# Two layers of a hybrid language model on one core: the head of the program regrouped, gates and squares scaled before the down projections, their sums added on VectorE, the last norm applied through row sums

## The reference

```python
def rmsnorm(x, g):
    xf = x.astype(jnp.float32)
    var = jnp.mean(xf * xf, axis=-1, keepdims=True)
    return (xf * lax.rsqrt(var + EPS) * g.astype(jnp.float32)).astype(x.dtype)
# first block, layer l
xn = rmsnorm(h, norm_mix_g[l])
u = jnp.einsum('bsd,de->bse', xn, w_in[l])
q, k, v, xr, gr, ga, gb = jnp.split(u, splits, axis=-1)
...
hn = rmsnorm(h, norm_ffn_g[l])
g, up = jnp.split(hn @ w_ffn_in[l], 2, axis=-1)
h = h + (jax.nn.silu(g) * up) @ w_ffn_out[l]
# second block, after each mixer, with a rmsnorm of its own:
#   h = h + relu(hn @ w_up) ** 2 @ w_down, and at the end rmsnorm(h, final_norm_g)
```

## Time and profile before

| | |
|---|---|
| time, median of 3 runs (lowest to highest) | 1148.96 us (1147.88 to 1152.42) |
| the profiled execution: its own time, its span | 1151.9 us, 1150.2 us |
| mean granted TensorE clock | 0.996 |
| busy: PE, DVE, ACT, POOL | 1121.5, 757.2, 573.3, 228.5 us |
| moved by DMA | 187.32 MB, mean 163 GB/s |

### The profile page before, as it was taken

How to read it: one execution, slowest core, us unless ns; L and a number is a source line. 1 busy time by engine, 2 the same in 40 slices (tenths; PEclk the granted TensorE clock), 3 DMA queues, 4 the chain that set the end, 5 groups by cost and what they waited for, 6 DMA issues and landing times.

```text
span 1150.2 us, 21081 instructions
## 1 busy us (share of the span) xinstructions
PE 1121.5 (98%) x8516; PEld 1070.6 (93%) x8516; DVE 757.2 (66%) x933; ACT 573.3 (50%) x747; POOL 228.5 (20%) x227
## 2 busy tenths in 40 slices
PE   6999999999999999999999999999989999999997
PEld 6999899999888899999999988899989999889996
DVE  5747884666777743699886777753367657776333
ACT  6346556635655543565664555543345445554331
POOL 1996001402000000267844010000030002000001
PEclk9999999999999999999999999999999999999999
DMA  9574433654665555446410355555545445555531
GB/s 282 178 250 145 161 112 111 219 181 151 204 197 184 182 189 180 142 131 195 154 38 2 111 183 182 186 197 179 181 134 183 147 148 183 183 182 188 181 142 37
DMA packets 154947, 187.32 MB, mean 163 GB/s; under 512 B 6496, under 2 KB 143872, under 8 KB 154880
## 3 DMA queue, kind: packets, MB, share of 16 engines
q1 hardware_dynamic: 151312, 184.06, 49.0%
q10 hardware_dynamic: 3568, 2.31, 0.7%
HBM read 185.29 MB, written 1.07 MB: 162 GB/s over the span
## 4 chain that ended last, share of the span: by engine, by line
PE 88%; DVE 8%; ACT 1%; DMA 1%; issue 1%; SPq 0%; POOLq 0%; POOL 0%; DVEq 0%
PE PS L441 17%; PE PS L383 17%; PE PS L384 17%; PE PS L385 17%; PE PS L443 9%; DVE WL L379 2%; DVE XHL L538 1%; PE PS L1936 1%; PE PS L1949 1%; PE PS L730 1%; DMA RAW<-in_w_in 1%; DVE QKV L1532 1%; PE PS L1898 1%; PE PS L680 1%; PE PS L1824 1%
## 5 line engine op out<-in xcount | busy, mean ns | idle before, releaser
L379 DVE TENSOR_TENSOR WL<-RAW,WH 128x2048 fp32r<-128x2048 f32 x171 | 400.5, 2343 | 215.9 <-ACT WH L370 215.9
L370 ACT ACTIVATE WH<-RAW 128x2048 fp32r<-128x2048 f32 x171 | 326.6, 1911 | 225.6 <-PE PS L385 206.9
L441 PE MATMUL PS<-XHL,WH 128*128 128x512 f32 x864 | 300.9, 395 | 0.0
L383 PE MATMUL PS<-XHL,WH 128*128 128x256 f32 x832 | 242.0, 291 | 13.6 <-DVE WL L332 6.9
L443 PE MATMUL PS<-XHL,WL 128*128 128x256 f32 x864 | 239.6, 277 | 0.0
L384 PE MATMUL PS<-XHL,WH 128*128 128x256 f32 x832 | 236.8, 285 | 0.0
L385 PE MATMUL PS<-XHL,WL 128*128 128x256 f32 x832 | 236.7, 284 | 0.0
L441 PEld LDWEIGHTS PS<-XHL,WH 128*128 128x128 f32 x864 | 162.1, 188 | 37.4
L383 PE MATMUL PS<-HH,WH 128*128 (+1 forms) x688 | 194.7, 283 | 0.0
L385 PE MATMUL PS<-HH,WL 128*128 (+1 forms) x688 | 194.7, 283 | 0.0
L384 PE MATMUL PS<-HL,WH 128*128 (+1 forms) x688 | 194.7, 283 | 0.0
(11 more groups left out here) (296 smaller groups left out, 1605.5 us busy)
## 6 DMA issues: line engine op xcount, KB each, us to landing
RAW<-in_mlp_w_up SPq DMA_DIRECT2D x32, 1024.0 KB, 5.4
RAW<-in_mlp_w_down SPq DMA_DIRECT2D x32, 1024.0 KB, 5.0
RAW<-in_w_in SPq DMA_DIRECT2D x26, 1024.0 KB, 5.2
RAW<-in_w_ffn_in_pairs SPq DMA_DIRECT2D x22, 1024.0 KB, 5.1
RAW<-in_dn_w_in SPq DMA_DIRECT2D x16, 1024.0 KB, 5.7
RAW<-in_mb_w_in SPq DMA_DIRECT2D x12, 1024.0 KB, 5.2
RAW<-in_w_ffn_out SPq DMA_DIRECT2D x11, 1024.0 KB, 5.0
RAW<-in_w_attn_out SPq DMA_DIRECT2D x4, 1024.0 KB, 5.3
```

The source lines that it names most:

```text
L370: act.activation(WH[:, k], RAW[:, k], ACT.Copy).then_inc(hi_done, 1)
L379: dve.tensor_tensor(WL[:, k], RAW[:, k], WH[:, k].bitcast(F32), ALU.subtract).then_inc(lo_done, 1)
L383: pe.matmul(out, wh, xh, start=start, stop=False, skip_group_check=True)
L441: pe.matmul(out.rearrange("p (e t) -> p e t", e=2), h[:, k, part], XHL[:, :, k], start=(k == 0), stop=False, skip_group_check=True)
```

## The change

The head: `xr` 2 is fetched and split in quarters too, `xr` 3 and `qk` 0 are fetched before the bias rows and `WRI`, ten matmuls of `ONES` are issued on PE as soon as `ONES` is set, ACT takes the norm's root before it splits `xr` 3, and DVE inverts it before its own split; the rows are made after the second quarter of `xr` 2. In the attention the low part of `gr` 1 is made between shift and scale of the first pair, that of `gr` 2 after its scale, and the scans come one chunk later. The decay rows get banks 6, 7, 4, 5 and are made together ahead of `dq` 9; the key and query sums move to banks 6 and 7. In `fi` both halves, and in `u0` and `u1` the relu, are multiplied by the rows before the product or the square (ACT squares twice: rounded, and in full), `ROWS_AT` for `u0` and `u1` goes from 5 to 3, and the down projections' banks are added to `H` by DVE directly. `w1` has its last block in bank 4, so that the last pair of blocks is finished block by block; the last norm has its sums in token columns, its root on two columns, and its rows through PE.

```diff
+        WARM = 10
+            pe.wait_ge(s_.const, 1)
+            for _ in range(WARM):
+                pe.matmul(PS[:, 7, 0:P], ONES[:], ONES[:], start=True, stop=True)
             for st in (Step(seg["xr"], j, None) for j in range(4)):
-                if st.j < 2:
+                if st.j < 3:
                     multiply_pieces(pe, st)
...
+                if c == 2 and p == 1:
+                    norm_point(pe, 0, 4)
...
-            for p in range(4):
-                fetch_piece(sp, 1, p)
-            fetch(sp, Step(seg["xr"], 2, None))
+            for c in (1, 2):
+                for p in range(4):
+                    fetch_piece(sp, c, p)
+            fetch(sp, Step(seg["xr"], 3, None))
+            fetch(sp, Step(seg["qk"], 0, None))
             sp.wait_ge(s_.ext_ready, 1)
...
             for st in (Step(seg["xr"], j, None) for j in range(4)):
-                split_hi(act, st)
                 if st.j == 1:
                     norm_root(act, 0)
+                if st.j:
+                    split_hi(act, st)
...
-                split_lo(dve, st)
-                attn_scale(dve, ch, n)
+                if n:
+                    split_lo(dve, st)
+                    attn_scale(dve, ch, n)
+                else:
+                    split_lo(dve, Step(seg["v"], 3, None))
+                    attn_scale(dve, ch, n)
+                    split_lo(dve, st)
...
-                if n < 4:
-                    scan(n)
+                if 0 < n < 5:
+                    scan(n - 1)
...
-        ROWS_AT = [4, 3, 2, 5, 3, 5]
+        ROWS_AT = [4, 3, 2, 3, 3, 3]
...
+        def add_rows(dve, sg, m):
+            for b in range(4 if m != FINAL else 3):
                 if b < 3:
                     dve.wait_ge(s_.rows_done, 3 * h4_no[sg.name] - 2 + b)
                 else:
                     dve.wait_ge(mm_done, sg.first + sg.n)
-                dve.tensor_tensor(XN[:, 2 * b:2 * b + 2, :], PS[:, b, :].rearrange("p (c t) -> p c t", c=2), by_rows(2),
-                                  ALU.mult).then_inc(s_.rows_scaled, 1)
-                if b > 1 and m != FINAL:
-                    norm_low(dve, m, b - 2)
                 hb = H[:, 2 * b:2 * b + 2, :]
-                ins = pool.tensor_tensor(hb, hb, XN[:, 2 * b:2 * b + 2, :], ALU.add)
+                ins = dve.tensor_tensor(hb, hb, PS[:, b, :].rearrange("p (c t) -> p c t", c=2), ALU.add)
...
+                if b and m != FINAL:
+                    norm_low(dve, m, b - 1)
...
+            dve.wait_ge(s_.rows_done, 3 * h4_no[sg.name] + 1)
+            dve.tensor_tensor(H[:, KB - 2], H[:, KB - 2], PS[:, 3, 0:TOK], ALU.add).then_inc(s_.h4, 1)
+            dve.wait_ge(mm_done, sg.first + sg.n)
+            dve.tensor_tensor(H[:, KB - 1], H[:, KB - 1], PS[:, 4, 0:TOK], ALU.add).then_inc(s_.h4, 1)
...
+                def square_of(st):
+                    k = slot_of(st, -1)
+                    act.wait_ge(s_.sg_in, st.local(base_ - 1))
+                    act.activation(hid(HH, st, 2, 1), two(SG[:, k]), ACT.Square).then_inc(s_.hh_done, 1)
+                    act.wait_ge(s_.hl_done, st.local(base_ - 4))
+                    act.activation(HP[:, k], SG[:, k], ACT.Square).then_inc(s_.hp_done, 1)
...
             def decay_rows(g):
-                if g >= 2:
-                    pe.wait_ge(s_.b_read, g - 1)
                 pe.wait_ge(s_.gc_done, 1)
-                rows_of(GC, 4 * g, 6 + g % 2).then_inc(s_.b_done, 1)
+                rows_of(GC, 4 * g, GB[g]).then_inc(s_.b_done, 1)
...
+        def final_pieces(act):
+            for p in range(3):
+                norm_high(act, FINAL, p)
+                if p < 2:
+                    final_scaled(act, p)
+            for j in (KB - 2, KB - 1):
+                act.wait_ge(s_.h4, h4_no["w1"] + j - (KB - 2))
+                act.activation(XN[:, j], H[:, j], ACT.Square).then_inc(s_.sq_done, 1)
+            final_scaled(act, 2)
+        def final_scaled(act, p):
+            for j in (2 * p, 2 * p + 1):
+                ins = act.activation(OUTG[:, j], H[:, j], ACT.Copy, scale=weight(FINAL, j))
+            ins.then_inc(s_.outg, 1)
...
-            ch(dve.reciprocal(RSTD[:], RH[:]))
-            ch.wait(dve)
+            dve.reciprocal(RC[:, 0:2], SDC[:, 0:2]).then_inc(s_.rc_ready, 1)
+            dve.wait_ge(s_.rows_ready, FINAL + 1)
             for p in range(4):
...
+                blk = slice(2 * p, 2 * p + 2)
+                dve.wait_ge(s_.outg, p + 1)
+                dve.tensor_tensor(XN[:, blk], OUTG[:, blk], PS[:, 5, None, 0:TOK].to_broadcast([P, 2, TOK]),
+                                  ALU.mult).then_inc(s_.xout, 1)
```

More of the change, by code:

```diff
@@ L252, in build @@
         x_in = [sem(f"x_in{p}") for p in range(4)]
-        piece_in = [sem(f"piece_in{p}") for p in range(6)]
+        piece_in = [sem(f"piece_in{p}") for p in range(9)]
         hi_done = sem("hi_done")
@@ L465, in multiply_rows @@
                 xl = HL[:, bass.ds(st.rel * KROWS + k, 1), :].rearrange("p k t -> p (k t)")
-                mm = product(pe, PS[:, b // 2, (b % 2) * TOK:(b % 2 + 1) * TOK],
+                if st.seg.name == "w1" and b == KB - 1:
+                    if first and k == 0:
+                        c = seg["u1"].first + seg["u1"].n - 1
+                        pe.wait_ge(freed[c % SLOTS], c // SLOTS + 1)
+                    out, opens = PS[:, 4, 0:TOK], first and k == 0
+                else:
+                    out, opens = PS[:, b // 2, (b % 2) * TOK:(b % 2 + 1) * TOK], first and k == 0 and b % 2 == 0
+                mm = product(pe, out,
                              h[:, k, b * P:(b + 1) * P], l[:, k, b * P:(b + 1) * P], xh, xl,
-                             first and k == 0 and b % 2 == 0, last and k == KROWS - 1)
-                if last and b % 2 and b < KB - 1 and k == KROWS - 1:
+                             opens, last and k == KROWS - 1)
+                if last and b < KB - 1 and k == KROWS - 1 and (b % 2 or st.seg.name == "w1" and b == KB - 2):
                     mm.then_inc(s_.rows_done, 1)
@@ L556, in norm_sums @@
             if m == FINAL:
[L557 to L560, removed]
+                pe.wait_ge(s_.sq_added, 6)
+                for j in (0, 1, 4, 5, 6, 7):
+                    if j >= 4:
+                        pe.wait_ge(s_.sq_done, 4 * m + max(j - 2, 3))
+                    for c in range(TT):
+                        mm = pe.matmul(PS[:, 6 + c, 0:P], XN[:, j, c * P:(c + 1) * P], ONES[:], start=(j == 0), stop=(j == 7),
+                                       skip_group_check=True)
             elif m == 2:
@@ L580, in norm_root @@
             elif m == FINAL:
-                act.activation(RH[:], PS[:, 4, 0:TOK], ACT.Sqrt, bias=EPSC[:], scale=1.0 / D).then_inc(s_.sd_done, 1)
+                act.activation(SDC[:, 0:2], PS[:, 6:8, 0], ACT.Sqrt, bias=EPSC[:], scale=1.0 / D).then_inc(s_.sd_done, 1)
             else:
@@ L819, in _ @@
                                  a[w].rearrange("(j e) d f -> e d j f", e=2)[e]).then_inc(s_.wri_in, 16)
-            fetch(sp, Step(seg["xr"], 3, None))
-            for name, n in SEGMENTS[1:]:
+            for st in (Step(seg["qk"], j, None) for j in range(1, 8)):
+                fetch(sp, st)
+            for name, n in SEGMENTS[2:]:
                 steps(sp, seg[name], lambda st: fetch(sp, st))
@@ L1015, in add_halves @@
             dve.tensor_tensor(two(SG[:, st.slot]), two(SG[:, st.slot]), wide_sides(st)[0], ALU.add).then_inc(freed[st.slot], 1)
-        def squares_ready(earlier):
-            def ready(act, st):
-                act.wait_ge(s_.hp_done, st.local(earlier - 1))
-            return ready
         @block.scalar
@@ L1040, in _ @@
             squares(act, 0, 3)
+            for p in range(4):
+                split_hi_piece(act, 2, p)
             def late_inputs():
@@ L1406, in _ @@
             for st in (Step(seg["xr"], j, None) for j in range(4)):
+                if st.j == 0:
+                    for p in range(4):
+                        split_lo_piece(dve, 2, p)
+                    continue
+                if st.j == 1:
+                    norm_inverse(dve, 0)
                 split_lo(dve, st)
-                if st.j == 0:
-                    continue
                 if st.j == 1:
@@ L1509, in up @@
                 dve.wait_ge(freed[st.slot], st.uses())
-                dve.tensor_tensor(SG[:, st.slot, 0:TOK], SG[:, st.slot, 0:TOK], RSTD[:], ALU.mult).then_inc(s_.sg_in, 1)
+                dve.tensor_tensor(two(SG[:, st.slot]), two(SG[:, st.slot]), by_rows(2), ALU.mult).then_inc(s_.sg_in, 1)
                 if st.i is not None or st.j >= 1:
@@ L2078, in _ @@
             norm_sums(pe, FINAL)
+            pe.wait_ge(s_.rc_ready, FINAL + 1)
+            for c in range(TT):
+                mm = pe.transpose(PS[:, 5, c * P:(c + 1) * P], RC[:, c:c + 1].to_broadcast([P, P]), IDENT[:])
+            mm.then_inc(s_.rows_ready, 1)
 _VECTORS = [name for name, _ in VECTORS]
```

112 lines of the change are left out of this document (55 added, 57 removed).

## The result

The changed kernel takes 1134.67 us (median of 4 runs, 1133.43 to 1135.08), against 1149.81 us for the kernel before beside it (4 runs, 1147.88 to 1152.42): a ratio of 0.9867, interval 0.9855 to 0.9879, or 15.1 us less. The forecast was 1129.5 in a range of 1125.0 to 1136.0; the sign and the range hold, the range by 1.3 us, and the size was overrated by a quarter. The profiled execution of the changed kernel has a span of 1133.4 us and an own time of 1135.08, 0.4 above its median. That of before stood some 2.1 above the median given here, so the two spans differ by 16.8 us where the medians differ by 15.1.

What follows compares the result with a forecast made beforehand. PE, busy 98% of the span, was taken as the bound. Gains of 5.4 + 3.6 + 7.2 + 1.1 + 4.2 = 21.5 us cut the span from 1150.2 to 1128.7; the median forecast was 1129.5, range 1125 to 1136.

Steps and rivals of the forecast that it cites:

- The head's wait and its low clock: Head: PE's wait for the norm's rows and the low clock after it go, gaining 5.4 us, bounds 1.5 and 6.2.
- the first pair's: First head pair: PE's 2.05 us wait and the 1.5 us low clock go, together 3.6 us, bounds 1.8 and 3.8.
- `fo`'s waits: End of `fo`: two of PE's six waits for low parts go, gaining 2.2 us of the down projections' 7.2.
- the decay rows': Decay rows: the 1.09 us wait goes but PE next waits for ACT's squares; gain 1.1 us, bounds 0.4 and 1.7.
- No wait of PE over 0.2 us between 7 and 550 us: One of the signs that would show the prediction right, for PE between 7 and 550 us.
- 1.8 us of `ROWS_AT`: Earlier `ROWS_AT`: root, half sums and inverse take some 1.8 us of DVE's 2.8; cost 0, at worst 0.5 twice.
- The step that failed: `w0`: End of `w0`: four of PE's six waits for low parts go, with a later one on `mq` 1, gaining 5.0 us.
- The tail: End of the kernel: finishing the last blocks and norm sooner gains 4.2 us, bounds 3.0 and 5.0.
- (a): Rival: a handoff behind the old wait takes its place, above all in the head; about 1136 us, chance 0.22.
- (b): Rival at the start: the ten dummy matmuls hold the clock up; 1128.7 us, chance 0.10.
- (c): Rival: PE's stalls don't add up, as DVE keeps its old times in `dq` and `dz`; 1140 us, chance 0.03.
- (d): Rival: slower, as the squares of `u0` and `u1` close a ring within a chunk; about 1210 us, chance 0.02.

Runs made afterwards that it cites:

- sums on DVE: The changed kernel with the sums of squares after `w0` (norm 4) on DVE and no longer on POOL: 1131.60 us, ratio 0.9841.
- the head alone: The kernel before with only the new order of the head, without dummies: 1146.23 us against 1149.69, ratio 0.9963.
- no dummies: The changed kernel without its ten dummy matmuls at the start: 1134.72 us, ratio 0.9866 to the kernel before.
- fewer sums: The changed kernel with DVE adding squares of blocks 1 to 0 and 5 to 4, so the last norm's sums take 16 records, not 24: 1133.90 us, 0.9856.
- the third square: The changed kernel with one more ACT square, into a tile nothing reads, in each chunk of `u0` and `u1`: 1134.55 us, ratio 0.986.
- pair alone: The kernel before with only the new order around the first head pair: 1145.86 us, ratio 0.9971.

## Why the prediction was right, and where its sum was off

**Right, by the runs.** PE was what bound the kernel, and the change paid where PE had stood still or run slowly. The head's wait and its low clock went (5.2 of 5.4 at `xr` 3), the first pair's too (3.5 of 3.6, and 3.5 when it was done alone), `fo`'s waits (2.4 of 2.2), the decay rows' (0.9 of 1.1, and 0.9 when undone). The new queue of transfers in the head cost nothing, nor did the doubled scaling in `fi` or the squares on ACT in `u0` and `u1`. "No wait of PE over 0.2 us between 7 and 550 us" failed by one wait, that of 0.3 us for a convolution, which the prediction had named among the signs of being wrong. How the gain of a place divides among the edits made there together (fetches, quarters and order in the head; blocks, columns and scaling in the tail) was not taken apart. The table load that the prediction packs into 1.8 us of `ROWS_AT` takes 1.28 us by itself in the trace; no wait came of it. And its count of the low windows, "17 and 16 matmuls start", is of those that overlap them: 15 and 14 start.

**The step that failed: `w0`, 5.0 predicted, 2.9 measured.** The prediction laid the new chain of DVE's adds and low parts against PE's quarters and found a lead of 1 us. It priced the low parts as with POOL idle, since the row adds were gone. POOL's adds of squares stayed. Before, DVE's low parts met POOL's instructions at this place and the two splits behind them did not (they start at 852.44 and take 4.48 us together). The prediction had the row in hand: low parts of 1.2 us beside POOL and of 0.41 without it. It did not ask who would stand beside the split of `mq` 1. Moved to DVE, those adds gave back 2.5 us, the missing 2.1 and 0.4 over.

**The tail, 4.2 predicted, 2.5 measured: the sums were mis-sized.** The prediction has the last square at 1139.0 and PE's sums done by 1139.5, 0.5 us later. They ended 2.05 us later, 1.5 more: the twelve matmuls take two records each, 24, and 2.94 us, and they begin only 0.9 us ahead of the last square's end. The trace of before has the same two records for each matmul of its last sums (L560: eight matmuls, 16 records). The rest is the end: from DVE's last multiply (1130.25) to the end of the span it is 3.1 us and not 2.6. The waits that were named went, and the 12.4 us from PE's last big matmul to the end became 9.9 and not 8.

**The head, 5.4 predicted, 4.6 measured at `v` 0.** The margin in front of the eighth gate was named as the rival's place. POOL did start 2.6 us earlier, but its convolutions took 2 us more in this execution, since one more of their instructions met one of DVE's splits. Groups of POOL's instructions from 20 to 90 us, before and after:

```profile
L862 POOL TENSOR_TENSOR XN<-XN,TAP 128x256 f32<-128x256 f32 x24 | 23.5, 981 | 2.0
L860 POOL TENSOR_SCALAR TAP<-XR,VEC 128x256 f32<-128x256 f32 x24 | 23.4, 975 | 2.3
L857 POOL TENSOR_SCALAR XN<-XR,VEC 128x256 f32<-128x256 f32 x8 | 4.4, 553 | 23.9 <-DVE XR L1366 23.2
```

```profile
L891 POOL TENSOR_TENSOR XN<-XN,TAP 128x256 f32<-128x256 f32 x24 | 19.7, 821 | 2.0
L889 POOL TENSOR_SCALAR TAP<-XR,VEC 128x256 f32<-128x256 f32 x24 | 17.4, 723 | 2.3
L886 POOL TENSOR_SCALAR XN<-XR,VEC 128x256 f32<-128x256 f32 x8 | 16.3, 2036 | 20.8 <-DVE XR L1403 20.0
```

23.5 + 23.4 + 4.4 = 51.3 us became 19.7 + 17.4 + 16.3 = 53.4, with nine stretched instructions before and ten after. The eighth ended at 84.90, 0.6 earlier than before, and PE came 5.2 earlier: the margin of 4.2 was used up. The tenth is the last add of the eighth convolution, which began 0.15 us behind a split (82.02). In the trace with the sums on DVE the same add began 0.05 us ahead of the split and was not held. First the changed kernel, then that one:

```profile
82.17 2.73 POOL L891 TENSOR_TENSOR XN<-XN,TAP 128x256 f32<-128x256 f32 x1
```

```profile
81.60 0.74 POOL L891 TENSOR_TENSOR XN<-XN,TAP 128x256 f32<-128x256 f32 x1
```

Of the eleven traces that have the new head, seven wait about 0.3 us at the eighth or the seventh gate and four do not (the head alone, no dummies, sums on DVE, fewer sums); there the eighth convolution was done 1.8 us ahead of PE, near the 1.5 of the prediction. So these 0.55 us are a matter of which instruction comes first, and not of every execution.

**The rivals.** (a) is what took the difference: a handoff behind the old wait came out at the convolution, and twice at `mq`. At 1134.67 the result lies nearer to its 1136 than to the 1129.5 of the forecast, and 0.22 was too little for it. Its detail was off: none of `w0`'s old waits stayed, others took their place. (b): with ten dummies the clock was up early in four of seven traces; fourteen started `v` 0.9 and 1.4 us earlier in two, for 0.7 us of median that lies within the spread, and without any the median is the same. A burst ahead of the work thus shows at its place and hardly in the time. The prediction had sized the burst wrongly: ten dummies fill 4.63 us and not 2, and leave PE idle for 1.4 and not 3, for they too take two records each, at the low clock. (c) did not occur: what was gained before `dz` was still there behind it. (d) is ruled out by the third square.

**From sum to median.** The prediction said that the median would fall by 18.5 to 21.5. It fell 1.7 less than the span, because the profile of before stood 2.1 above its median and that after only 0.4. The profile with the pair alone shows the old head 2.9 us quicker in another execution, which would account for it. The mean granted clocks of the 31 further executions of before speak for it: the ten at 0.994 or 0.995 took 1150.7 to 1152.8 us, the other 21, at 0.996 to 0.998, took 1147.6 to 1150.2 but for one of 1152.3. Which wait those executions had was not traced, so that part stays open. Before spreads over 4.5 us, the changed kernel over 1.7.

## What to carry to other kernels

When a wait goes, list what else runs on the engines of that place in the new order, and above all whether GpSimd and VectorE now read SBUF at the same moment: four cheap instructions left on GpSimd cost this kernel 2.5 us, and on VectorE they cost it nothing. Size matmuls of fp32 from a row that shows their records, not from the spacing of another kind. Judge a part of under 1 us by the first matmul of the chunk behind it, not by the time of the kernel.

## What the runs showed of the hardware

- A matmul of 128 columns in fp32 takes two records of some 0.11 us at the upper clock (24 in 2.94 us) and of 0.21 at the lower (20 in 4.63). With 16 columns the records are 0.11 us apart as well.
- A burst of ten matmuls that ends 1.0 to 1.9 us before the work left the clock low until 10.1 to 10.6 us in three executions and had it up at 4.2 to 5.9 in four others, in one of which it fell again. Fourteen, which reach up to the work or to 0.3 us before it, had it up from the first real matmul on in both traces. Without a burst it rose at 10.3 to 12.8 in four.
- PE's waits of 2.90 and 1.89 us were each followed by 3.4 us at the low clock; a wait of 1.72 us at the first of the two places was not (pair alone).
- DVE's splits beside POOL's adds took 3.39 and 3.37 us instead of 2.29, and POOL's adds up to 3.22 instead of 1.3. A POOL add that began 0.15 us behind a split took 2.73 instead of 0.74.
